# A hybrid encoder layer on one Trainium2 core: the fill of the empty expert slots and six subtractions issued at other places

## What is computed

```
h = rmsnorm(x, g_mix);  z = h @ w_in                      # 1024 -> 8192
m = sig(g_r) * (silu(r_g) * Ret(h)) @ w_ret_o + sig(g_d) * Diff(h) @ w_diff_o
x = x + m @ w_out
h = rmsnorm(x, g_ffn)
group = argmax(h @ w_group + b);  2 experts of 4 in it, softmax weights
x = x + sum over the 2 experts e of weight * (silu(h @ w_gate[e]) * (h @ w_up[e])) @ w_down[e]
```

## Time and profile before

| | |
|---|---|
| median of three runs | 1140.6 us |
| profiled execution: its time, its span | 1142.49 us, 1140.7 us |
| TensorE busy, mean granted clock | 1036.9 us (91%), 0.967 |
| VectorE, ScalarE, GpSimd busy | 647.5, 514.1, 155.1 us |
| HBM read, written | 199.05 MB, 47.09 MB |
| SyncE's DMA queue (q1) | 162.25 MB, 37.2% of 16 engines |
| GpSimd's DMA queue (q0) | 74.19 MB, 20.1% |

### The profile page before, as it was taken

The page is one execution under the profiler, slowest core; times in us unless marked ns, Lnnn a source line. Parts: engine busy times, 40 slices in busy tenths (PEclk is TensorE's granted clock), DMA queues, the critical chain, the costliest instruction groups (busy, mean ns, idle before and its releaser), DMA issues.

```text
span 1140.7 us, 12143 instructions
## 1 busy us (share of the span) xinstructions
PE 1036.9 (91%) x4736; PEld 835.2 (73%) x4736; DVE 647.5 (57%) x897; ACT 514.1 (45%) x690; POOL 155.1 (14%) x179
## 2 busy tenths in 40 slices
PE   4979399999999999999999999999299999999993
PEld 3767378787777776777787788787178888888882
DVE  4645367514443444333343754767688888988870
ACT  3521123333443434432335031345458787877851
POOL 1000002011021020111013000001202121212111
PEclk9999799999999999999999999999599999999997
DMA  9253445545245161344146454225799999999962
GB/s 309 71 199 148 168 164 188 169 166 198 86 161 168 64 232 48 127 141 152 57 168 226 173 184 148 74 82 179 267 415 366 377 406 385 400 390 390 400 232 40
DMA packets 59890, 237.31 MB, mean 208 GB/s; under 512 B 5328, under 2 KB 5504, under 8 KB 47216
## 3 DMA queue, kind: packets, MB, share of 16 engines
q1 hardware_dynamic: 39088, 162.25, 37.2%
q0 software_dynamic: 20736, 74.19, 20.1%
HBM read 199.05 MB, written 47.09 MB: 216 GB/s over the span
## 4 chain that ended last, share of the span: by engine, by line
PE 81%; DMA 10%; DVE 3%; ACT 2%; issue 2%; POOL 1%; SPq 0%; ACTq 0%; DVEq 0%; POOLq 0%
PE ps L441 20%; PE ps L443 20%; PE ps L442 20%; DMA raw<-in_w_in 7%; PE ps L1608 3%; PE ps L1609 3%; PE ps L1624 2%; PE ps L1584 2%; DMA q_tok<-z_q 2%; PE ps L1758 2%; PE ps L1661 1%; PE ps L1869 1%; PE ps L1690 1%; PE ps L1741 1%; PE ps L1772 1%
## 5 line engine op out<-in xcount | busy, mean ns | idle before, releaser
L441 PE MATMUL ps<-w_hi,s_hi 128*128 128x512 f32 x672 | 272.4, 405 | 29.0 <-issue 27.7
L442 PE MATMUL ps<-w_hi,s_lo 128*128 128x512 f32 x672 | 264.6, 394 | 0.0
L443 PE MATMUL ps<-w_lo,s_hi 128*128 128x512 f32 x672 | 264.5, 394 | 0.0
L441 PEld LDWEIGHTS ps<-w_hi,s_hi 128*128 128x128 f32 x672 | 128.1, 191 | 58.3 <-issue 30.0
L395 DVE TENSOR_TENSOR w_lo<-raw,w_hi 128x2048 fp32r<-128x2048 f32 x42 | 96.2, 2290 | 97.6 <-ACT w_hi L390 97.4
L443 PEld LDWEIGHTS ps<-w_lo,s_hi 128*128 128x128 f32 x672 | 127.9, 190 | 27.5
L442 PEld LDWEIGHTS ps<-w_hi,s_lo 128*128 128x128 f32 x672 | 128.2, 191 | 26.8 <-issue 1.0
L848 ACT ACTIVATE stage<-ps,x_rstd 128x512 f32<-128x512 f32 x64 | 44.0, 689 | 198.8 <-PE ps L443 198.8
L390 ACT CAST w_hi<-raw 128x2048 fp32r<-128x2048 f32 x42 | 80.0, 1908 | 66.3 <-DMA raw<-in_w_in 61.1
L751 POOL DMA_INDIRECT out_y<-y_exp,s_idx x16 | 45.9, 2869 | 231.7 <-ACT y_exp L1069 231.7
L413 DVE TENSOR_TENSOR lo_x<-raw_x,w_hi 128x2048 fp32r<-128x2048 f32 x32 | 71.9, 2284 | 3.8 <-ACT w_hi L408 3.8
(11 more groups left out here) (282 smaller groups left out, 1759.4 us busy)
## 6 DMA issues: line engine op xcount, KB each, us to landing
raw<-in_w_in SPq DMA_DIRECT2D x32, 1024.0 KB, 8.1
raw_x<-in_w_up SPq DMA_DIRECT2D x30, 1024.0 KB, 12.2
raw_x<-in_w_down SPq DMA_DIRECT2D x18, 1024.0 KB, 12.3
raw<-in_w_gate SPq DMA_DIRECT2D x16, 1024.0 KB, 11.2
raw_x<-in_w_gate SPq DMA_DIRECT2D x16, 1024.0 KB, 12.8
raw<-in_w_down SPq DMA_DIRECT2D x14, 1024.0 KB, 10.8
x_slots<-in_c_empty SPq DMA_DIRECT2D x4, 2112.0 KB
x_exp<-x_slots POOLq DMA_DIRECT2D x16, 528.0 KB, 13.0
```

The source lines that it names most:

```text
L441: nc.tensor.matmul(out, s_h, w_h, start=first, stop=False)
L442: nc.tensor.matmul(out, s_l, w_h, start=False, stop=False)
L443: return nc.tensor.matmul(out, s_h, w_l, start=False, stop=last)
```

## The change

The four fills of expert slots go out behind blocks 32 to 35 instead of 4 to 7, the spare rows behind block 36 instead of 8, and the sink rows behind those instead of ahead of block 2. In routing, `rows_of_tile` runs ahead of `choose`; the splits of the first expert's blocks 2 and 3 run one tile earlier, at the third and fourth tile; the splits of blocks 4 and 5 on VectorE come behind the counts and behind a new wait for all scatters (`dispatched`). Nothing else differs, and no instruction is added or taken away but that wait.

```diff
@@ -505,15 +505,16 @@
         sp.dma_start(x_tok[0:SAMPLE, PT, :], a["x_sample"][0]).then_inc(x_in[PT], 16)
-        sp.dma_start(y_dram[SINK:SINK + P, :], a["c_empty"][:, 0:D_MODEL]).then_inc(y_init, 16)
         for n in range(2, N0):
             dense_load(n)
-            if 4 <= n < 4 + NG:
-                e = EPG * (n - 4)
+            g = n - BPC * IN_CHUNKS
+            if 0 <= g < NG:
+                e = EPG * g
                 sp.dma_start(x_slots[e * CAP:(e + EPG) * CAP, :].rearrange("(e c) x -> e c x", e=EPG)[:, 0:P, :],
                              a["c_empty"].unsqueeze(0).to_broadcast([EPG, P, XW])).then_inc(slots_empty, 16)
-            elif n == 4 + NG:
+            elif g == NG:
                 sp.dma_start(x_slots[PAD:PAD + P, :], a["c_empty"]).then_inc(slots_empty, 16)
+                sp.dma_start(y_dram[SINK:SINK + P, :], a["c_empty"][:, 0:D_MODEL]).then_inc(y_init, 16)
@@ -1032,8 +1033,8 @@
-            if n >= 3:
-                split_hi(act, 0, 0, n - 1)
+            if n in (2, 3):
+                split_hi(act, 0, 0, n)
             if n:
                 exps(ORDER[n - 1])
@@ -1475,20 +1476,17 @@
             evacuate_out(4, t)
             if n:
                 root_of_tile(ORDER[n - 1])
+                rows_of_tile(ORDER[n - 1])
                 choose(ORDER[n - 1])
             evacuate_out(5, t)
-            if n:
-                rows_of_tile(ORDER[n - 1])
-            if n >= 3:
-                split_lo(dve, 0, 0, n - 1)
+            if n in (2, 3):
+                split_lo(dve, 0, 0, n)
         place_rows(ORDER[PT - 1])
...
         choose(ORDER[PT])
         place_rows(ORDER[PT])
-        split_lo(dve, 0, 0, 4)
-        split_lo(dve, 0, 0, 5)
...
         own(v.tensor_scalar(slot_row[:, :], base16, -float(PAD), None, ALU.add))
+
+        dve.wait_ge(dispatched, 16 * 2 * TT)
+        split_lo(dve, 0, 0, 4)
+        split_lo(dve, 0, 0, 5)
```

## The result

The changed kernel takes **1153.57 us** (median of five runs, 1151.37 to 1155.1); the kernel before, beside it, 1140.6 (1139.87 to 1144.69). The ratio is 1.0103, 95% interval 1.0086 to 1.0119: 12 us slower by the ratio and 13 by the medians, where 7 us faster were forecast. The profiled execution took 1154.33 us with a span of 1152.5, 11.8 more than before, at a mean granted clock of 0.958 (before 0.967). The time lies 2 us above that of the third rival, 1151.5.

The account below looks back on a forecast made before the run. Fills on four DMA engines hold up the loads and gates queued behind or beside them, and TensorE stands idle. -33.6 (early) + 32 (middle) - 5.5 (tail) = -7.1 us: median 1133.5, whole range 1122 to 1153.

Parts of the forecast that it names:

- third rival: Middle: the last `rg` gate falls behind the fourth fill, whole at 680 to 681, shift 50; 1151.5 us, chance 0.17.
- Early part: Chunks 0 to 4: the fills cost 33.6 us there, and moving them brings all of it back.
- First shift: Chunk 15: block 33, whole only at 603.5 behind fill 1, stops TensorE 7 us, plus 2 for lower clock: 9.
- The failed step: Middle: the second `gd` gate, issued at 623, starts at 625, in time to alternate with block 34 (625 to 633).
- shift of the middle: Chunks 15 to 18: delay from the moved fills, mainly VectorE's wait for `rg` (30), then block 36; 32 us in all.
- its own side: The forecast's case: a shift of 27 to 36 in the middle, 1128.5 to 1137.5 us, chance 0.60.
- half-way: Middle: the gate lands inside fill 4, shift 38 to 46, 1139.5 to 1147.5 us, chance 0.10.
- Tail: Routing after the last tile: `choose` starts 4.2 us sooner, scatters and row loads change too; sum -5.5, bounds -3 to -7.
- -2.4 + 0.5 + 0.6: Routing's end: last two scatters without L413 beside them -2.4, loads in flight +0.5, first row load beside L413 +0.6.
- Rivals 1 and 2: First: chunks 15 to 18 cover the fills, 1101.5, chance 0.03; second: only the fills' queue is held up, 1109.5, 0.10.
- the order's own hope: Middle: chunks 15 to 18 cover the fills, so the move costs nothing there; 1101.5 us, chance 0.03.
- rival 1: Middle: chunks 15 to 18 cover the fills; -33.6 - 5.5 gives 1101.5 us, chance 0.03.

Follow-up runs that it names:

- spread kernel: The changed kernel with each fill written as 16 outer pieces, over sixteen DMA engines, at the same places of the queue: 1113.81 us, ratio 0.9748.
- Run 4: The changed kernel with the fourth fill behind block 36 and the pad and sink rows behind block 37: 1148.26 us, ratio 1.0065.
- run 8: The changed kernel with the splits of blocks 4 and 5 right behind the last place_rows, without their wait for the scatters: 1154.78 us, ratio 1.0114.
- run 5: The changed kernel with each fill as two copies of 4 x 64 rows of 4.2 KB, on the same four engines: 1149.58 us, ratio 1.0066.

## Why the prediction was wrong

**Early part: right.** -33.6 of -33.6 by the interval that it named. (The 52.4 us of the earlier trace rows were five waits: blocks 5 to 7 had 41.7 of them, the two splits behind these 10.7.) 1.6 us were lost again in chunk 6 (32.65 us from tile 4 to tile 4, 31.09 before), in the spread kernel as well; why is open.

**First shift: right.** Block 33 was to be whole at 603.5 - 32.7 = 570.8; ScalarE's split of it began at 571.25, behind 14.6 us of waiting. The `gd` gate's second half went out at 591.09, against 614.05 - 32.7 = 581.35: a shift of 9.7 where 9 was reckoned.

**The failed step** is the one that follows: "The second `gd` gate, issued at 614.05 + 9 = 623, starts at 625, in time to alternate with block 34 (625 to 633)." The margin was said to be three packets and 3 us. I had block 34's share on the four engines take 8 us, a packet of GpSimd for each of its 32 pieces, and all of this gate's 20 packets among them. By the prediction's own steps, less 32.7, that is from 592.3 to 600.3. The trace has a record of 4 bytes at the end of each transfer on each engine. On the four engines those of fill 2 come at 591.4 to 592.9, as stepped, those of block 34 at 594.9, 595.7, 596.0 and 598.3 and those of fill 3 at 616.9 to 620.4. So block 34 needed 3.5 to 4.1 us on three of the four engines and 5.4 on the fourth. For part of that time GpSimd's queue was still at the last `gr` store, issued at 588.68, ahead of the gate, and whole 6.2 us later at 594.9; the stepping had not put it there. The DMA of 596 to 600 us in the changed kernel, where the forecast still had block 34, shows fill 3 at work:

```profile
q1 hardware_dynamic: 17, 0.36, 21.4%
```

Seven of these 17 packets are pieces of 49 KB. The gate's own 4-byte records come at 612.5 on the one engine and at 619.0 to 619.5 on the three, where block 35 had by then begun behind fill 3. At one packet per piece of fill 3, eleven of the gate's 20 packets went beside fill 3 on these three, and the time left for block 35's turns gives it some five to nine of the rest: an estimate that leaves none to four beside block 34, where the forecast had 20. Why no more of them found a turn there, once the store was out, is open.

In the list of DMA issues (KB, median us to landing) block 34, the second half of `gd` and the two halves of `rg` read (the first half of `rg` was there for the L1344 at 624.99, the second for the one at 648.44):

```profile
raw<-in_w_diff_o SPq DMA_DIRECT2D x1, 1024.0 KB, 14.3
...
gate<-z_gd POOLq DMA_DIRECT2D x1, 1280.0 KB, 28.8
...
gate<-z_rg POOLq DMA_DIRECT2D x2, 1280.0 KB, 40.6
```

Fill 3 and block 35 had no turns left for the second half of `rg`, and all of fill 4 went ahead of it, as the third rival has it: "whole at 680 to 681", on this kernel's axis 647.3 to 648.3 against a measured 648.44, and shift 50 against 51. Run 4 shows that it was the fourth fill: with it out of the way the gate is whole at 630.51.

Was it a mis-sized term or a wrong picture? The picture of four engines, whole turns of 1.81 us and about one GpSimd packet between them held beside all the fills. What failed is the turn-taking with the 2 KB pieces of block 34: the shift of the middle, put at 32, measured 49.8 (51 less the 1.2 regained). Between the third and the fourth fill the result jumps by 18 us, and the forecast stood 2 us and three packets from the jump, on an alternation that no row showed; yet it gave its own side 0.60 and the far side 0.17, with 0.10 half-way. The rival's condition was also put too far off: the first shift need not exceed 12 us, 9.7 was enough, since block 34 had mostly gone through.

**Tail: right in its sum, in part by luck.** -5.5 forecast, -4.95 measured in the profile. The start of `lt` came 3.6 us sooner, not 4.2 (7.21 us behind the last eviction, 10.83 before): TensorE ran its 16 router matmuls at a pitch of 0.21 us and not 0.11, at the lower of its two levels, as before. In the twin of run 8 the pitch was 0.11 and the gain the full 4.2 (6.60). The scatters and row loads gave 1.3, the sum of -2.4 + 0.5 + 0.6, but not by these terms. The first scatter's issue was 1.5 us shorter, as reckoned; from the second's issue to the landing passed 4.66 us, where 3.5 had been forecast and 4.35 measured before; and the row loads lost nothing beside L413 (run 8), where 0.6 had been put down. The first miss, less the 0.5 allowed for it, and the second cancel.

**Rivals 1 and 2** fell with the order's own hope: chunks 15 to 18 cover a fill on four engines no better than chunks 2 to 4 do. But 1101.5, rival 1's time for fills that hold nothing up, is what the fills over sixteen engines reached (1102.6 and 1103.4).

## What to carry to other kernels

Read how many DMA engines a transfer runs on before deciding where to put it: a share of 0.25 in a window that holds nothing else means four, and then everything that is queued behind it or beside it waits on those four, wherever it stands; here the shape of the copy was worth 28 to 40 us and its place between a loss of 15 and a gain of 8, both on four engines. A transfer that is moved out of one stall lands in front of something else, so list what is issued on both queues at the new place and ask of each when it is wanted. Where a forecast rests on which of two queues gets the next few turns, and one more missed turn costs a whole 20 us transfer, give both sides of that edge about equal chances, however exact the stepping looks.

## What was not expected of the hardware

- The length of one queue's pieces sets the other queue's share. Against 49 KB pieces GpSimd's 4 KB packets got about one turn per 1.8 us and engine; against 4.2 KB pieces the two queues shared the engines by halves (13 of 25 pieces per us), and the third fill took 37 us.
- With many small pieces SyncE itself stood at the issue. In the kernel of run 5 the issue of block 35 and the one of the next fill's two copies lasted 20 and 18 us, against 0.4 and 1.4 for the first of their kind, so later blocks were not even in the queue. SyncE's timeline of that kernel:

```profile
596.07 19.83 SPq L493 DMA_DIRECT2D raw<-in_w_diff_o  x1
615.93 18.01 SPq L514 DMA_DIRECT2D x_slots<-in_c_empty  x2
```

  In the changed kernel the fourth fill's issue took 5.22. That the descriptors had no room is my reading; no run tested it.
- While TensorE stood for the gate, its granted clock was 0.50 in the rows, and the slices that hold the pause show .6 in place of .9. Behind the 2 us pause ahead of the router matmuls (window of 816.5 to 819.3 us) it was 0.54 in the changed kernel and 0.81 in the kernel of run 8, whose engines did the same up to there; `lt` came 0.6 us later for it.
